# Opening products in passes, a mean that TensorE subtracts, and a memory step that begins with its scores

## What is computed

```python
for layer in range(2):
    if layer == 0:
        z = x @ a_w_in; zu = gelu(z[:, :768]); zv = layer_norm(gelu(z[:, 768:1536])); qm = z[:, 1536:]
        mix = zu * (causal(w_s) @ zv + b_s)            # within chunks of 128 tokens, per head
    else:
        kvf = x @ kv_w                                 # keys, values, forget logits
        logcum = cumsum(log_sigmoid(kvf[:, 1536:] + kv_b_f))
        z = x @ b_w_q; q = z[:, :768]; qm = z[:, 768:]
        mix = softmax(q k^T / 8 + logcum[t] - logcum[s], causal) v
    mk, mv = mem @ mem_w_kv[layer]                     # 4 heads of 64 over 256 memory tokens
    mo = softmax(qm mk^T / 8) mv
    x = layer_norm(ALPHA * x + concat(mix, mo) @ w_o[layer])
    x = layer_norm(ALPHA * x + relu(x @ w_up[layer])**2 @ w_down[layer])
```

## Time and profile before

| | |
|---|---|
| three runs, us | 1173.68, 1175.94, 1175.03; median 1175.03 |
| profiled execution, us | 1173.03 |
| its span, us | 1171.2 |
| busy, TensorE / its weight loads | 1144.9 us (98%) / 967.9 us (83%) |
| busy, VectorE / ScalarE / GpSimd | 632.2 us (54%) / 489.0 us (42%) / 130.5 us (11%) |
| chain that ended last | TensorE 84%, VectorE 5%, ScalarE 4%, unexplained issue 4%, DMA 1%, GpSimd 1% |

### The profile page before, as it was taken

How to read it: one execution, slowest core, us unless ns; L and a number is a source line. 1 busy time by engine, 2 the same in 40 slices (tenths; PEclk the granted TensorE clock), 3 DMA queues, 4 the chain that set the end, 5 groups by cost and what they waited for, 6 DMA issues and landing times.

```text
span 1171.2 us, 16350 instructions
## 1 busy us (share of the span) xinstructions
PE 1144.9 (98%) x5785; PEld 967.9 (83%) x5785; DVE 632.2 (54%) x1076; ACT 489.0 (42%) x847; POOL 130.5 (11%) x153
## 2 busy tenths in 40 slices
PE   8999989999999999999999999999999999999997
PEld 8888879888888888889778888789888888888886
DVE  6668757444233454445587778866444223444226
ACT  6556338443122343224765565536434122333220
POOL 4000045000000000233300010055000000000000
PEclk9999989999999999999999999999999999999999
DMA  7213323233333333333212222133233333333332
GB/s 305 76 62 100 95 68 90 73 106 91 108 90 90 101 97 102 96 90 91 66 43 58 69 54 56 53 107 91 72 92 105 95 102 90 90 90 106 92 109 89
DMA packets 163798, 107.22 MB, mean 92 GB/s; under 512 B 4642, under 2 KB 156194, under 8 KB 163620
## 3 DMA queue, kind: packets, MB, share of 16 engines
q1 hardware_dynamic: 163172, 104.18, 29.7%
q10 hardware_dynamic: 576, 2.36, 0.6%
HBM read 104.43 MB, written 2.10 MB: 91 GB/s over the span
## 4 chain that ended last, share of the span: by engine, by line
PE 84%; DVE 5%; ACT 4%; issue 4%; DMA 1%; POOL 1%; SPq 0%; DVEq 0%; ACTq 0%; POOLq 0%
PE proj L580 68%; PE pv L580 3%; PE sc L580 2%; PE sc L953 2%; PE proj L953 2%; PE pv L953 2%; PE tr L953 2%; PE tr L627 1%; DVE w_lo L1558 1%; ACT w_hi L1168 1%; DMA w_raw<-in_mem_w_kv 1%; POOL total L2173 1%; DVE sc L1627 1%; ACT x L1345 0%; DVE probs L1646 0%
## 5 line engine op out<-in xcount | busy, mean ns | idle before, releaser
L580 PE MATMUL proj<-x_hi,w_hi 128*128 128x512 f32 (+1 forms) x752 | 292.8, 391 | 3.2 <-DVE w_lo L1558 1.6
L1558 DVE TENSOR_TENSOR w_lo<-w_raw,w_hi 128x1024 fp32r<-128x1024 f32 (+1 forms) x168 | 210.5, 1253 | 154.0 <-ACT w_hi L1168 105.9
L580 PE MATMUL proj<-x_hi,w_lo 128*128 128x512 f32 (+1 forms) x752 | 288.0, 384 | 0.0
L580 PE MATMUL proj<-x_lo,w_hi 128*128 128x512 f32 (+1 forms) x752 | 282.5, 383 | 0.0
L1168 ACT CAST w_hi<-w_raw 128x1024 fp32r<-128x1024 f32 x153 | 159.9, 1045 | 201.4 <-PE proj L580 198.2
L580 PEld LDWEIGHTS proj<-x_hi,w_hi 128*128 128x128 f32 x752 | 142.2, 189 | 30.8 <-ACT x_hi L1347 2.5
L580 PEld LDWEIGHTS proj<-x_hi,w_lo 128*128 128x128 f32 x752 | 142.2, 189 | 28.1
L580 PEld LDWEIGHTS proj<-x_lo,w_hi 128*128 128x128 f32 x752 | 139.2, 188 | 25.0
L580 PE MATMUL proj<-h_hi,w_hi 128*128 128x512 f32 (+1 forms) x384 | 146.3, 381 | 0.4 <-DVE w_lo L1558 0.4
L580 PE MATMUL proj<-h_lo,w_hi 128*128 128x512 f32 (+1 forms) x384 | 146.0, 380 | 0.0
L580 PE MATMUL proj<-h_hi,w_lo 128*128 128x512 f32 (+1 forms) x384 | 146.0, 380 | 0.0
(11 more groups left out here) (365 smaller groups left out, 1822.8 us busy)
## 6 DMA issues: line engine op xcount, KB each, us to landing
w_raw<-in_w_up SPq DMA_DIRECT2D x64, 512.0 KB, 4.0
w_raw<-in_w_down SPq DMA_DIRECT2D x64, 512.0 KB, 3.6
w_raw<-in_w_o SPq DMA_DIRECT2D x16, 512.0 KB, 3.6
w_raw<-in_a_w_in SPq DMA_DIRECT2D x12, 512.0 KB, 3.3
w_raw<-in_kv_w SPq DMA_DIRECT2D x12, 512.0 KB, 3.9
w_raw<-in_b_w_q SPq DMA_DIRECT2D x8, 512.0 KB, 3.6
w_raw<-in_mem_w_kv SPq DMA_DIRECT2D x5, 512.0 KB, 3.5
x<-in_x SPq DMA_DIRECT2D x4, 512.0 KB, 10.3
```

The source lines that it names most:

```text
L580: last = pe.matmul(target, lhs, rhs, start=start and n == 0, stop=stop and n == len(terms) - 1)
L1558: return dve.tensor_tensor(target, whole, hi.bitcast(F32), ALU.subtract)
```

## The change

Five things are changed. (1) The warming products are 13 of 512 columns instead of 26 of 128. (2) In the opening, unit 1, the memory values and the first query unit are made in three passes over the eight input tiles instead of three products per tile; the first pass waits only for high parts. ScalarE casts unit 2 before it copies the first keys. (3) The copies of the memory keys to the other head's rows (layer 0) go from ScalarE to GpSimd, ahead of its `trunk_lo`. (4) In both out projections the provisional mean is taken off tiles 2 to 7 by one more product with a matrix of -1/128 (`minus_r`) and `shift_in`; VectorE's separate subtraction there goes. (5) In the double step the first scores come before any filler, then two fillers of four tiles; `prepare` of the first step's second unit is put ahead of the forget gate's logarithm on ScalarE, and `f_sp`, `lf_hi`, `lf_lo` are put into the step's units 0 and 1.

```diff
-    WARM = 26
+    WARM = 13
...
             def project(b, g, hi, lo, columns=T, order=range(KT), ready=None, parts=(0, KT),
-                        start=True, stop=True):
+                        start=True, stop=True, shifted=False):
...
+                if shifted and parts[1] == KT:
+                    last = products(bank[:, 0:columns], [(minus_r[:, :], shift_in[:, :])], False)
...
+            def by_passes(b, g, bank, passes):
+
+                wait(pe, proj_free[g.slot], g.half())
+                for n, (signal, count, each, pairs) in enumerate(passes):
+                    pe.wait_ge(signal, count)
+                    for k, (lhs, rhs) in enumerate(pairs):
+                        if each:
+                            each(k)
+                        last = pe.matmul(bank, lhs, rhs, start=n == 0 and k == 0, stop=n == len(passes) - 1 and k == KT - 1)
+                last.then_inc(w_used, 1)
+
+            def opening_projection(b, g, hi, lo, hi_there=None, lo_there=None, columns=T):
+
+                wh, wl = weights(b)
+                tiles = range(KT)
+                by_passes(b, g, proj[g.slot][:, 0:columns], (
+                    (w_hi_ready, b.base + 1, hi_there, [(wh[:, k], hi[:, k]) for k in tiles]),
+                    (w_split, b.base + 1, None, [(wl[:, k], hi[:, k]) for k in tiles]),
+                    (w_split, b.base + 1, lo_there, [(wh[:, k], lo[:, k]) for k in tiles])))
+
             def natural_values(m):
...
-                pe.wait_ge(w_split, b + 2)
-                wait(pe, proj_free[g.slot], g.half())
-                for k in range(KT):
-                    mh, ml = memt_hi[:, k, here], memt_lo[:, k, here]
-                    wh, wl = open_hi[:, 0:2, k, :], open_lo[:, 0:2, k, :]
-                    last = products(bank, [(mh, wh), (mh, wl), (ml, wh)], k == 0, k == KT - 1)
-                last.then_inc(w_used, 1)
+                tiles = range(KT)
+                by_passes(b, g, bank, (
+                    (w_hi_ready, b + 2, None, [(memt_hi[:, k, here], open_hi[:, 0:2, k, :]) for k in tiles]),
+                    (w_hi_ready, b + 2, None, [(memt_lo[:, k, here], open_hi[:, 0:2, k, :]) for k in tiles]),
+                    (w_split, b + 2, None, [(memt_hi[:, k, here], open_lo[:, 0:2, k, :]) for k in tiles])))
...
-                at = [0, 4, 6] if mixing else [0, 5, 7] if s.base == STEP_B else [0, 3, 6]
+                at = [0, 4, 6] if mixing else [0, 0, 4] if s.base == STEP_B else [0, 3, 6]
...
-                project(b.plus(2), g.plus(2), mix_hi, mix_lo, order=out_order, parts=(5, KT))
-                project(b.plus(3), g.plus(3), mix_hi, mix_lo, order=out_order)
+                project(b.plus(2), g.plus(2), mix_hi, mix_lo, order=out_order, parts=(5, KT), shifted=True)
+                project(b.plus(3), g.plus(3), mix_hi, mix_lo, order=out_order, shifted=True)
...
-            memory_projection(0, 1)
+            opening_projection(Pos(1), Pos(1), memt_hi, memt_lo, columns=M)
...
-            project(Pos(B_AQ), Pos(G_AQ), x_hi, x_lo, ready=trunk_ready)
+            opening_projection(Pos(B_AQ), Pos(G_AQ), x_hi, x_lo, lambda k: pe.wait_ge(x_hi_ready, k + 1), trunk_ready)
             project(Pos(B_AQ + 1), Pos(G_AQ + 1), x_hi, x_lo)
             pe.wait_ge(const_ready, 4)
+            pe.wait_ge(mk_copied, 2 * MEMPAIRS)
...
-                           [mk_twice[other_rows(head), 2 * c + head, :] for head in range(2)])
+                           [mk_twice[other_rows(head), 2 * c + head, :] for head in range(2)] if layer else None)
...
+                    if double(s) and u == 0:
+                        act.wait_ge(f_step, 4)
+                        act.wait_ge(lf_zeroed, 2)
+                        for r in range(0, P, 32):
+                            last = act.copy(lf_hi[:, :, r:r + HEADS], f_sp[:, :, :])
+                        last.then_inc(f_act, 1)
...
             prepare(Pos(1))
+            prepare(Pos(2))
             memory_projection(0, 0)
-            prepare(Pos(2))
             prepare(Pos(3))
...
             memory_values()
+            prepare(Pos(B_FOX + 1))
...
+                    if double(s) and u == 0:
+                        dve.wait_ge(f_step, 3)
+                        dve.wait_ge(f_act, 2)
+                        dve.tensor_tensor(f_sp[:, :, :], f_ln[:, :, :], f_neg[:, :, :], ALU.add).then_inc(f_step, 1)
+                    if double(s) and u == 1:
+                        dve.wait_ge(f_step, 4)
+                        dve.wait_ge(lf_zeroed, 2)
+                        dve.wait_ge(f_act, 3)
+                        for r in range(0, P, 32):
+                            last = rest(lf_lo[:, :, r:r + HEADS], f_sp[:, :, :], lf_hi[:, :, r:r + HEADS])
+                        last.then_inc(f_step, 1)
...
                 for j in range(2, 4):
-                    shifted_residual(n, Pos(b + j), Pos(g + j), Pos(j))
+                    residual(n, Pos(b + j), Pos(g + j), Pos(j))
...
                 for j in range(4, 6):
-                    pre_shift(n, j)
                     prepare(Pos(b + j + 2))
                     part_residual(n, b + j, j, 0)
...
-                for j in range(6, KT):
-                    pre_shift(n, j)
...
+            dve.memset(minus_r[:, :].bitcast(F32), -1.0 / P).then_inc(const_r, 1)
...
+            for c in range(MEMPAIRS):
+                pool.wait_ge(qk_hi, Q_MEM[0] + c + 1)
+                for head in range(2):
+                    own = 2 * c + head
+                    pool.tensor_copy(mk_twice[other_rows(head), own, :], mk_twice[own_rows(head), own, :]).then_inc(mk_copied, 1)
+                    pool.wait_ge(mk_copied, own + 1)
```

69 lines of the change are left out of this document (28 added, 41 removed).

## The result

The changed kernel took 1163.17 us (median of four, 1163.01 to 1165.02) against 1175.49 us for the kernel before, measured beside it (1173.68 to 1177.36): a ratio of 0.9899, 95% interval 0.9880 to 0.9918. The forecast was 1169.2 us with a range from 1165.4 to 1172.9, so the sign was right and the size was not: the gain was forecast at 5.8 us. Timed again on other occasions the changed kernel came out at 0.9929 (0.9915 to 0.9943) and 0.9911 (0.9898 to 0.9925); over all 76 executions of the kernel before and 15 of the changed one the medians are 1173.8 and 1164.3 us. The two profiled executions, 1173.03 and 1163.30 us, differ by 9.7 us (spans 1171.2 and 1161.6).

What follows compares the result with a forecast made beforehand. TensorE's own work, busy 1144.9 of 1171.2 us, was taken as the bound, plus waits and half-clock stretches. Terms -2.0 - 2.0 - 1.5 - 0.9 + 0.6 = -5.8 us from 1175.03 gave 1169.2 us, range 1165.4 to 1172.9.

Steps and rivals of the forecast that it cites:

- the clock's: Behind layer 0's out projection: part of the 3.2 us lost at half clock comes back, taken as 1.5 us.
- Rival 2: Clock wholly back behind layer 0's out projection: 1.7 us more gain, 1167.5 us; chance 0.15.
- The base: Whole kernel: median of three runs 1175.03 us, 2.0 us above the profiled 1173.03 us; the gain was subtracted from the median.
- Opening: Opening up to the first query product: x_hi starts at 14.7 instead of 16.7 us, 2.0 us gained; bounds 0.9 to 2.9.
- rival 4: Opening: the key copies on GpSimd hold VectorE's splits and x_lo, gain there only 0.5 us, 1170.7 us; chance 0.11.
- Layer 0: Layer 0's out projection: sums 2.5 us earlier, 0.48 us of added products bare, together -2.0 us; gain at most 3.6.
- The term of +0.48 for the second half: Layer 0's out projection, second half: four added products of 0.120 us lie bare, costing 0.48 us.
- Double step: Double memory step, first turn: table load and TensorE's resumption come earlier, -0.9 us; bounds -0.3 to -1.3.
- Layer 1: Layer 1's out projection: first half ends 0.55 us later, second half's 0.48 us nearly all vanish; +0.6 us, bounds 0 to +1.4.
- 1 (clock stays slow): Half-clock stretches behind layer 0's out projection remain, 1.5 us less gain, 1170.7 us; chance 0.15.
- 3 (VectorE isn't what frees TensorE): GpSimd and ScalarE hold layer 0's chain, gain there 0.2 us instead of 2.0, clock stays slow: 1172.5 us; chance 0.13.
- 5 (the clock falls at new places): Clock falls over layer 1's sums and at the feed-forwards' ends, four stretches more at 1.6 us each: 1177.1 us; chance 0.04.

Runs made afterwards that it cites:

- kernel with filled pauses: The kernel before with 8, 8 and 4 idle products of 512 columns in TensorE's three pauses of layer 0's out projection: 1172.28 us, ratio 0.9990.
- kernel with spare subtractions: The changed kernel with VectorE's six scaled subtractions of layer 0's out projection done anyway, into an unread tile: 1169.59 us against 1163.94 us.

## Why the prediction was wrong, step by step

- **The step that failed is the clock's.** The prediction put "between 0 and 3.2 us, and take 1.5, the middle, for want of a row that decides". What came back is the whole stretch, 2.7 us where 1.5 was put: the segment behind layer 0's sums is 2.71 us shorter, and it is 404.4 to 404.7 us in each of the eleven profiles without a fall there. The price was right too as far as it goes. Up to layer 0's second sums the stretch costs 3.1 us (17.88 us against 14.77 in the kernel with filled pauses); a wait behind them takes up some 0.4, so 2.7 reach the forget gate. The middle stood for no case: in a single execution a fall is there or not. And the count of falls was short. The profile has one more at 808.9 us, which the sum never lists; behind layer 1's second sums the profiled pair differs by 1.79 us, of which such a fall was measured at 1.2, and 0.6 stay open. Luck is in it as well, since the changed kernel's other profiles have a fall at 800 us; and one in the opening and one at the double step occur in other executions of the same kernel, which a single profile can't show. Rival 2, clock wholly back, was nearest, and its 1167.5 us was still too high: it lacks the fall at 808.9 us too, and the rest is the base.
- **The base.** "The median is 2.0 us above it" was taken as a constant to add. It is the offset of a group of three. Over 76 executions the kernel before has its median at 1173.8 us, 0.8 above the profiled one; the changed kernel's, 1164.3, is 1.0 above its own. So a constant between profile and median was sound here, but its size was chance, and it hid that the group measured beside the change was high as well. Some of the difference between executions is falls (opening, double step) that this profile lacked and the change removes; in the medians the fall near 800 us stands against them.
- **Opening**: right, with part of the gain in another place. The query product was forecast at about 21.3 and started at 21.40; x_hi at 14.7, it was 15.12, only 1.6 us earlier. The other 0.3 us came on the path that the prediction names, VectorE's queue: its split of x_lo takes 1.31 us instead of 1.60, and the low part of the memory values, behind which the bank is free, comes 1.9 us earlier than before (22.78):

```profile
15.12 2.18 ACT L1474 CAST x_hi<-x 128x512 fp32r<-128x512 f32 x4
```
```profile
17.34 1.31 DVE L1585 TENSOR_TENSOR x_lo<-x,x_hi 128x512 fp32r<-128x512 f32 x1 [0.45 <-ACT x_hi L1474]
...
20.92 0.42 DVE L1585 TENSOR_TENSOR mv_lo<-proj,mv_hi 128x256 fp32r<-128x256 f32 x1
```

  The four copies took GpSimd 2.3 us and not 1.4, and rival 4 is out all the same: the two splits of 128x1024 beside them took 2.36 us as before (from 13.64 us on, and from 14.16 before). The price of the fall, some 1.2 us in part of the executions, is the term that lacked.
- **Layer 0**: right in its steps. In old times TensorE was to resume at 154.25, 158.75 and 162.3 and come to the sums at 165.8; less the opening's 2.0 that is 152.25, 156.75, 160.3 and 163.8, and the trace has 152.43, 156.78, 160.30 and 163.42. The split that GpSimd's sum of squares was to hold up started and ended as forecast (155.9 and 158.3 in old times):

```profile
154.00 2.31 DVE L1585 TENSOR_TENSOR split_lo<-w_raw,split_hi 128x1024 fp32r<-128x1024 f32 x1
```

  The gain is 3.05 in the profiled pair and 3.6 between the groups (131.5 and 127.9), since this profile of the kernel before was quick here (131.09 of 131.1 to 132.2). "The first stretch costs nothing now" held: 131.53 us in the kernel with spare subtractions, which had no fall at that place. The term of +0.48 for the second half was 0: those products are 0.47 us more up to the second sums (15.24 against 14.77) and gone in a wait behind them (404.62 against 404.65 us without them). That the segment's -2.71 is also 3.2 less 0.48 is luck: both are cut by that same wait.
- **Double step**: -0.98 for -0.9. **Layer 1**: +0.64 and +0.14 for +0.6 (+0.4 for the first in the mean of the seven profiles and the five); the 0.48 us that I let vanish "nearly all" vanished in layer 0, not here.
- **Rivals**: 1 (clock stays slow) was wrong: with the pauses the falls of layer 0 went, in eight of ten profiles. The Trainium skill, TensorE: Matmul & The Clock Gate, section "HAM oscillation", named beside that rival, warns of longer pauses only. The trace differs: half clock stood behind pauses of 1.88, 1.82 and 0.96 us, and filling them kept it away. 3 (VectorE isn't what frees TensorE) fell with the spare subtractions. 5 (the clock falls at new places) didn't come: in the changed kernel's three profiles the only fall ahead of the end is the one near 800 us, where the kernel before has one too (808.9).

## What to carry to other kernels

Write down every stretch at half clock in the trace, TensorE busy or not, and price each by itself: 1.2 to 1.7 us for 3.4 us where TensorE was the bound here, at most 0.2 where it waited, nothing where it had finished. Then ask of each whether the change takes away the pause ahead of it, and give the term its whole price or none, each with a chance; half is no case of its own. Look at several executions' clocks before trusting one profile's count. Where VectorE set the stage (layer 0), the work moved to TensorE cost nothing, and where VectorE had room (layer 1) nearly its full length, 1.3 of 1.4 us; move it stage by stage.

## What the runs showed of the hardware

- Half clock often follows pauses of TensorE of 1 to 3 us, and idle products in the pauses kept it away (58 instructions at 1.00 for 37 at 0.58 in 6.8 us, mean clock 0.9949 for 0.9928). In layer 0 six of six profiled kernels with VectorE's operations and open pauses (the longest 1.7 to 3.0 us) fell, five of them behind the sums; of ten without these operations and with pauses of at most 1.2 us, two did. That the one-column products beside the pauses matter was supposed and not tested.
- Whether it falls is not decided by the program alone: the same rows at 799 us ran at both clocks, and executions of the kernel before have mean clocks from 0.989 to 0.996. What decides it stays open.
- The granted clock explains the spread of executions only in part: 0.53 us for each 0.001 of the mean over 76 executions, where a stretch that TensorE pays in full would give 1.17 us (0.001 of 1171). Some falls lie where nobody waits for TensorE, and some of the spread is other waits: in two of eighteen profiles TensorE stood 0.7 and 0.9 us for a late weight near the end.
- Idle products are not free to place: in the kernel before the stage with them took 132.4 us up to the sums instead of 131.1 to 132.2, and the whole gained 0.1% where 0.4% was expected. I didn't find by which wait.
